# GpSimd makes a stage's first weight sums in the stage before, and junctions take their second half in another order

## The reference

```python
h = rms_norm(x, g_pre_mix) * (1 + scale1) + shift1
proj = h @ w_in                               # keys, values, queries, Fourier and conv inputs, gates
merged = sum(sigmoid(gate_b) * (branch_b @ w_br_b) for b in four branches)
x = x + gate1 * rms_norm(merged @ w_out, g_post_mix)
h = rms_norm(x, g_pre_mlp) * (1 + scale2) + shift2
x = x + gate2 * rms_norm(square(relu(h @ w1)) @ w2, g_post_mlp)
```

## Time and profile before

| what | value |
|---|---|
| median of 3 runs | 4097.98 us (4097.63 to 4100.86) |
| profiled execution | 4095.34 us, span 4093.4 us |
| TensorE busy | 3808.4 us, 93% |
| VectorE busy | 1895.3 us, 46% |
| GpSimd busy | 1026.2 us, 25% |
| ScalarE busy | 833.0 us, 20% |
| mean granted TensorE clock | 0.972 of full |

### The profile page before, as it was taken

How to read it: one execution, slowest core, us unless ns; L and a number is a source line. 1 busy time by engine, 2 the same in 40 slices (tenths; PEclk the granted TensorE clock), 3 DMA queues, 4 the chain that set the end, 5 groups by cost and what they waited for, 6 DMA issues and landing times. The chain is left out here.

```text
span 4093.4 us, 47789 instructions
## 1 busy us (share of the span) xinstructions
PE 3808.4 (93%) x18222; PEld 2592.6 (63%) x18222; DVE 1895.3 (46%) x3491; ACT 833.0 (20%) x1685; POOL 1026.2 (25%) x876
## 2 busy tenths in 40 slices
PE   6978969999989989999998999999999999979998
PEld 5866735555465557555554555555787777768887
DVE  3345332222322266787544566655225655144445
ACT  2123221111111155211213000001213511220001
POOL 1301200000014211223332223232152034434443
PEclk9988989999999999999999999999999999999999
DMA  5410179999811100122221232221110012212221
GB/s 204 178 69 16 63 289 393 395 391 395 328 36 52 47 11 8 55 91 87 88 90 41 93 116 111 103 103 52 47 63 31 10 63 75 90 62 83 83 88 57
DMA packets 72014, 476.64 MB, mean 116 GB/s; under 512 B 8240, under 2 KB 9648, under 8 KB 18288
## 3 DMA queue, kind: packets, MB, share of 16 engines
q1 hardware_dynamic: 68576, 462.86, 29.9%
q0 software_dynamic: 2640, 8.65, 0.7%
q10 hardware_dynamic: 576, 2.10, 0.1%
HBM read 469.38 MB, written 4.19 MB: 116 GB/s over the span
## 5 line engine op out<-in xcount | busy, mean ns | idle before, releaser
L921 PE MATMUL ps<-projected,weight_ring 128*128 128x384 f32 (+1 forms) x672 | 245.8, 521 | 0.0
L3410 PE MATMUL ps<-projected,weight_ring 128*128 128x384 f32 (+1 forms) x768 | 223.0, 434 | 1.2 <-DVE mlp_u L3608 0.6
L2322 DVE SCALAR_TENSOR_TENSOR sb_x_all<-ps,sb_modulation_ada,sb_x_all 128x512 f32<-128x512 f32 x144 | 106.5, 750 | 244.4 <-PE ps L2158 214.8
L921 PEld LDWEIGHTS ps<-projected,weight_ring 128*128 128x128 f32 x672 | 127.7, 190 | 106.1 <-issue 45.9
L3410 PEld LDWEIGHTS ps<-projected,weight_ring 128*128 128x128 f32 x768 | 144.8, 190 | 62.5 <-issue 3.0
L3410 PE MATMUL ps<-projected,mlp_weight_sums 128*128 128x384 f32 x512 | 176.4, 488 | 0.0
L1304 DVE TENSOR_REDUCE attention_shift<-ps 128x1 f32<-128x768 f32 (+1 forms) x160 | 130.9, 846 | 77.8 <-PE ps L1192 77.5
L1192 PE MATMUL ps<-projected 64*128 64x256 f32 (+1 forms) x576 | 136.9, 531 | 25.2 <-DVE projected L1333 15.1
L2844 DVE SCALAR_TENSOR_TENSOR projected<-projected,sb_vectors 128x497 f32<-128x497 f32 (+26 forms) x270 | 157.9, 650 | 1.6
L2704 PE MATMUL ps<-projected,gates_weight_sums 128*128 128x384 f32 (+1 forms) x512 | 151.9, 440 | 5.0 <-POOL gates_weight_sums L2984 5.0
L3410 PE MATMUL ps<-h2b,weight_ring 128*128 128x384 f32 (+1 forms) x512 | 151.0, 439 | 4.9 <-ACT h2b L834 4.9
(11 more groups left out here) (664 smaller groups left out, 7765.8 us busy)
## 6 DMA issues: line engine op xcount, KB each, us to landing
weight_ring<-w_stream SPq DMA_DIRECT2D x218, 1024.0 KB, 4.9
expert_weights<-w_moe SPq DMA_DIRECT2D x125, 1024.0 KB, 22.3
weight_ring<-w_moe SPq DMA_DIRECT2D x40, 1024.0 KB, 23.6
h2b<-w_moe SPq DMA_DIRECT2D x33, 1024.0 KB, 24.0
weight_ring<-w_stream SPq DMA_DIRECT2D x16, 512.0 KB, 3.7
weight_ring<-w_stream SPq DMA_DIRECT2D x16, 384.0 KB, 3.2
sb_x_all<-xT SPq DMA_DIRECT2D x1, 3072.0 KB, 11.9
tokens<-h_tokens ACTq DMA_DIRECT2D x4, 512.0 KB, 9.6
```

What stands on the lines that cost most here:

```text
L921: ins = nc.tensor.matmul(core.ps[:, 2 * slot + half, 0:n], w_of(k), h_of(k)[:, a:a + n], start=(first and k == 0), stop=(last and k == chu ...
L2322: v.scalar_tensor_tensor(core.x[:, k, NCTX:T], ps[:, bank, :], core.mods["ada"][:, 40 + k, 1:2], core.x[:, k, NCTX:T], ALU.mult, ALU.add). ...
L3410: ins = nc.tensor.matmul(acc, wq[:, k, :], bq[:, k, :], start=(first and k == 0), stop=(last and k == 3), skip_group_check=True)
```

## The change

GpSimd's first weight sums of `project`, `out` and `mlp` are made by the end of the stage before, in a buffer that outlives it: one unit for `project` and `out`, two for `mlp` (into chunks 9 to 14 of `pr`, for which other buffers of `out` and of the MLP's junction move). The stage that follows starts its own sums at unit 1 (at unit 2 in the MLP, without a wait for products until unit 4), and waits on counts shifted by that. `modulate_side` now stands before unit 2's sums and their weights' arrival. In every junction four adds of half 1 stand before half 0's norms instead of two; in the MLP the totals of half 1 stand before both `x_second` products, and all eight norms of half 1 before the first column sum.

```diff
@@ Junction.vector_begin
-        self.adds(dve, 1, 0, 2)
+        self.adds(dve, 1, 0, 4)
         for k in range(KD):
             self.norm(dve, 0, k)
-        self.adds(dve, 1, 2, KD)
+        self.adds(dve, 1, 4, KD)
@@ project_phase
                 jn.modulate_side(pool)
+            if ahead is not None:
+                weight_quarters(pool, ahead, stream.arrived(pool, len(units)), sums_ready, 0)
@@ gates_phase
-        sw = ph.sb("weight_sums", [P, 2, 4, 4, P])
...
                     .then_inc(m15_out, 1)
+            pool.wait_ge(products, 7 * (len(jobs) - 1))
+            weight_quarters(pool, sw[:, 0], stream.arrived(pool, 2 * len(jobs) + len(mods)), s_ready, len(jobs))
             for r in (1, 0):
@@ seven_phase
             for i in range(U):
-                w = stream.arrived(pool, i + min(burst * i, len(mods)))
-                if i >= 2:
-                    pool.wait_ge(products, 7 * (i - 1))
-                weight_quarters(pool, sw[:, i % 2], w, s_ready, i)
+                if i >= made:
+                    w = stream.arrived(pool, i + min(burst * i, len(mods)))
+                    if i >= 2:
+                        pool.wait_ge(products, 7 * (i - 1))
+                    weight_quarters(pool, sw[:, i % 2], w, s_ready, i - made)
                 pool.wait_ge(m1_out, i + 1)
...
+            for j in range(2 if ahead is not None else 0):
+                weight_quarters(pool, ahead[:, j], stream.arrived(pool, U + j), s_ready, U - made + j)
...
+            def sums(i, count):
+                if i >= made:
+                    pe.wait_ge(s_ready, 4 * (i - made) + count)
@@ mlp_phase
+        def weight_sums(i, k):
+            return (made if i < 2 else sw)[:, i % 2, k]
...
             jn.gate_gains(pool)
-            for i in range(units):
+            jn.modulate_side(pool)
+            for i in range(2, units):
                 w = stream.arrived(pool, i + min(max(i - 1, 0), len(mods)))
-                if i == 2:
-                    jn.modulate_side(pool)
-                if i >= 2:
+                if i >= 4:
                     pool.wait_ge(products, done(i - 2, 7))
...
             x_first(0, w0, lambda k: jn.normal(pe, 0, k))
+            jn.x_totals(pe, 1, 0, 1)
             x_first(1, w1)
-            jn.x_totals(pe, 1, 0, 2)
+            jn.x_totals(pe, 1, 1, KD)
             x_second(0, w0, lambda k: jn.normal(pe, 0, 4 + k))
-            jn.x_totals(pe, 1, 2, KD)
             x_second(1, w1)
...
-            for k in range(6):
+            for k in range(KD):
                 jn.norm(dve, 1, k)
             for j in range(2):
                 jn.normal(dve, j, 3)
             next(h_sums)
-            for k in range(6, KD):
-                jn.norm(dve, 1, k)
             for j in range(2):
                 jn.normal(dve, j, KD - 1)
             next(h_sums)
@@ second_block
+                prj = ExitStack()
+                sw = sb("weight_sums", [P, 2, 4, 4, P], prj)
...
-                project_phase(core, f"project_tokens{layer}", h, units, scaled=not last, join=join)
+                project_phase(core, f"project_tokens{layer}", h, units, scaled=not last, join=join,
+                              ahead=sw[:, 0])
...
+                sw = sb("gate_sums", [P, 2, 4, 4, P], mg)
...
+                made = pr[:, 9:17, :].rearrange("p c t -> p (c t)")[:, 0:32 * P].rearrange(
+                    "p (j i k m) -> p j i k m", j=2, i=4, k=4)
                 seven_phase(core, f"out{layer}", merged, span[0], n,
                             [(h[:, 2 * i, :], h[:, 2 * i + 1, :], False, 1.0) for i in range(4)],
-                            sums.rearrange("p (i k m) -> p i k m", i=3, k=4), tail=squares)
+                            sums.rearrange("p (i k m) -> p i k m", i=3, k=4), tail=squares, sw=sw, made=1, ahead=made)
```

More of the change, by code:

```diff
@@ L924, in feature_job, with project_phase @@
     return ins
-def project_phase(core, name, h, units, scaled=False, join=None):
+def project_phase(core, name, h, units, scaled=False, join=None, ahead=None):
     nc, stream = core.nc, core.stream
@@ L944, in project_phase @@
             early = sum(job[0] == "T" and job[4] < TILES // 2 for _, job in jobs)
+        sums_ready = ph.sem("weight_sums_ready") if ahead is not None else None
         owner = [0 if j < early else j % 2 for j in range(len(jobs))]
@@ L2620, in _, with gates_phase @@
                                         ALU.add).then_inc(high_out, 1)
-def gates_phase(core, name, layer, h, pr, merged, branches, span, mods=()):
+def gates_phase(core, name, layer, h, pr, merged, branches, span, sw, mods=()):
     nc, ps, stream = core.nc, core.ps, core.stream
@@ L3121, in add, with seven_phase @@
                 .then_inc(self.added, 1)
-def seven_phase(core, name, b, lo, n, units, th=None, conv=None, mods=(), burst=0, heads=None, tail=None):
+def seven_phase(core, name, b, lo, n, units, th=None, conv=None, mods=(), burst=0, heads=None, tail=None,
+                sw=None, made=0, ahead=None):
     nc, ps, stream = core.nc, core.ps, core.stream
@@ L3214, in _ @@
                     bg.turn(pe)
-                pe.wait_ge(s_ready, 4 * i + 1)
+                sums(i, 1)
                 pe.wait_ge(t_ready, 1)
@@ L3223, in _ @@
                     bg.turn(pe)
-                pe.wait_ge(s_ready, 4 * i + 3)
+                sums(i, 3)
                 pe.wait_ge(t_ready, 2)
@@ L3240, in _ @@
                 pe.wait_ge(m5_out, i + 1)
-                pe.wait_ge(s_ready, 4 * i + 4)
+                sums(i, 4)
                 product(z, s[:, 3], right(4, 1), False, True)
@@ L3326, in _, with mlp_phase @@
                     bg.add(dve)
-def mlp_phase(core, h, out, span, th, tail, hid, m1, join, mods=()):
+def mlp_phase(core, h, out, span, th, tail, hid, m1, join, made, mods=()):
     nc, ps, stream = core.nc, core.ps, core.stream
@@ L3436, in z_first @@
                     pe.wait_ge(z_out, i - 1)
-                product(banks(i)[2], sw[:, i % 2, 0], left(b, 0, lo + n), True, False)
+                product(banks(i)[2], weight_sums(i, 0), left(b, 0, lo + n), True, False)
             def y_first(i, w):
                 up, b, t, lo, ready, made = sides(i)
-                pe.wait_ge(s_ready, 4 * i + 3)
+                if i >= 2:
+                    pe.wait_ge(s_ready, 4 * i - 5)
                 pe.wait_ge(ready, made + 2)
@@ L3457, in y_second @@
                 pe.wait_ge(ready, made + 3)
-                product(banks(i)[1], sw[:, i % 2, 2], t[:, 1], False, False)
+                product(banks(i)[1], weight_sums(i, 2), t[:, 1], False, False)
             def z_second(i, w):
@@ L3462, in z_second @@
                 pe.wait_ge(m5_out, i + 1)
-                pe.wait_ge(s_ready, 4 * i + 4)
-                product(banks(i)[2], sw[:, i % 2, 3], left(b, 4, lo + n), False, True)
+                if i >= 2:
+                    pe.wait_ge(s_ready, 4 * i - 4)
+                product(banks(i)[2], weight_sums(i, 3), left(b, 4, lo + n), False, True)
             def y_third(i, w):
@@ L3926, in second_block @@
                 merged = sb("merged", [P, KD, T], mg)
+                sw = sb("gate_sums", [P, 2, 4, 4, P], mg)
                 gates_phase(core, f"gates{layer}", layer, h, pr, merged,
[L3928 removed]
+                            [(DQ, 4), (GQ, 4), (UF, 3), (UC + 3, 3)], span, sw, () if last else mod_units("mod0", 8, 24))
                 dump(f"merged{layer}", merged)
                 n = span[1] // 2
[L3931 to L3932 removed]
+                sums = pr[:, 17:23, :].rearrange("p c t -> p (c t)")[:, 0:12 * n]
+                squares = (pr[:, 4, span[0]:T], pr[:, 5:7, span[0]:T])
+                made = pr[:, 9:17, :].rearrange("p c t -> p (c t)")[:, 0:32 * P].rearrange(
+                    "p (j i k m) -> p j i k m", j=2, i=4, k=4)
                 seven_phase(core, f"out{layer}", merged, span[0], n,
                             [(h[:, 2 * i, :], h[:, 2 * i + 1, :], False, 1.0) for i in range(4)],
[L3935 removed]
+                            sums.rearrange("p (i k m) -> p i k m", i=3, k=4), tail=squares, sw=sw, made=1, ahead=made)
         cols = span[1]
```

22 lines of the change are left out of this document (11 added, 11 removed).

## The result

The changed kernel takes 4069.25 us (median of 4 runs, 4067.72 to 4071.29), the kernel before 4097.81 (4 runs, 4096.33 to 4100.86). The ratio is 0.9923, interval [0.991, 0.9935]. On the 4097.98 us that the prediction started from, that ratio is 4066.4 us (4061.1 to 4071.3 by the interval). The direction was right and most of the places too. The gain is larger than the range (4067 to 4085) allowed: by 0.6 us, which is within the noise, while the 10 us to the forecast of 4076 are not. The profiled executions are 4068.01 us (span 4066.1) against 4095.34 (4093.4): 27.3 us.

A forecast was written before the change was run, and what follows sets the result against it. TensorE, busy 93% of the span, was taken as the bound, so only its waits could be won. Terms 4.85 + 2.05 + 5.9 + 7.4 + 0.8 + 1.6 + 1.5 - 2.4 = 21.7 us gave 4076 us, range 4067 to 4085.

The forecast's parts named there:

- term of 3.25: Head of `project0`: without the wait for GpSimd's sums the third product starts 3.25 us earlier.
- 1.6 for the third product: Head of `project0`: with no idle time before it, the third product escapes the half clock, 1.6 us more gained.
- term of 2.05: Head of `out0`: the third product starts at 2133.1 instead of 2135.21, counted as 2.05 us gained.
- which stays: Head of `out0`: the second product (3.15 us) begins at the low clock, and this was taken to remain.
- 5.9 forecast: Head of `out1`: 4.6 us from waits gone plus 1.3 from the third product's clock, together 5.9 us gained.
- forecast 2.4: Tail of `out1`: GpSimd's eight sums made ahead end after the stage's old end, 2.4 us lost.
- rival on the tails: Tails of the out stages: sums at 2.77 us each and half-clock opening matmuls make the kernel slower, 4103; chance 0.03.
- 14.1: First MLP junction: norm to norm 10.8 us unheld, 14.1 with four sums each holding a VectorE operation about 0.8.
- bounds 0 to 1.2 lost: `project_tokens1`: norms start 1.2 us late, but the eighth multiply comes about when it came; taken as 0.
- No relief: Second MLP junction: GpSimd still makes eight sums at the start, only for other units, so 0 gained from them.
- I take half: First sum products of both MLPs: half the low-clock cost counted as gained, 0.8 us in the first, 1.5 in the second.
- more comes back: Rival: high clock from both MLPs' first sum product (2.3 us), adds slipping past unit 2's sums (3.3); 4071, chance 0.13.

The follow-up runs named there:

- own_sums1: The changed kernel, but `out1` makes no sums ahead and the second MLP forms those of units 0 and 1 at its start; 4067.48 us.
- hold: The changed kernel, but GpSimd forms the sums of units 2 and 3 only after the last product of units 0 and 1; 4062.51 us.
- again: A second execution of the unmodified changed kernel, for its trace; 4067.45 us.
- sums_alone: The changed kernel with the old order in all junctions, the sums still made ahead; 4080.91 us, ratio 0.9952 to the kernel before.
- order_alone: The kernel before with only the new order of the junctions, no sums made ahead; 4085.98 us, ratio 0.9963 to the kernel before.
- three_adds: `hold` with three adds of half 1 ahead of the norms instead of four, in all junctions; 4057.83 us.

## Why the prediction was off, step by step

**Heads.** `project0` became 5.0 us shorter in this pair of executions, 4.85 were forecast. But 1.7 of it is clock that before's second execution did not lose; the wait itself is worth 3.3. So the term of 3.25 is right, and that the 1.6 for the third product came too was luck. `out0`: the term of 2.05 is right where the first product is at the low clock on both sides: in `own_sums1` the third product starts at 2129.56, 8.17 us after the first, against 10.20, 2.03; what was won of it is the wait of the earlier trace rows and a little. I took the low clock there as given ("which stays"); in the changed kernel and those that share its program up to there it was there in full, in part or not at all, and `gates0` and `out0` together fell by 2.2 to 6.6 us, 4.9 in the profiled pair. That the gain came out larger than the sum is luck as far as this term goes. `out1`: 6.3 measured without the tail (358.6 to 352.3), 5.9 forecast.

**Tails.** 2.2 us in `out1` (forecast 2.4), 0 in `out0` (0). All sixteen sums took 1.26 to 1.28. The low clock behind the wait, which I had only in the rival on the tails, came in `out1`'s tail in one of the two executions (5.46 against 2.91).

**First MLP.** Forecast 8.2, measured 8.5, and two of its parts were wrong in opposite ways. The start of the norms came 6.4 us earlier (6.2). Norm to norm fell by 0.9 (1.7): I had made 14.1 out of VectorE's adds held by four sums, but with the new order these cost nothing (`hold`), and 1.7 of the 14.92 is the low clock of a first product that now waits 3.71 us. The pair of sum products gave 1.6 us, of which I had taken half.

**project_tokens1.** Forecast 0 with bounds 0 to 1.2 lost; it gained 1.2. This is a wrong sign: I saw that the eighth multiply would come when it had come, and missed that the job before it no longer halted at the seventh. Its price lay outside the bounds that I gave. That the sums cost nothing there is true only with the order; alone they cost 2.4.

**Second MLP.** Forecast 3.1, measured 5.9 (6.8 in `again`). The sum products gave 2.8 us (6.51 to 3.72), of which 1.5 was taken; norm to norm gave 1.9 (12.79 to 10.86) for 1.6; 0.5 is an early wait of unit 1 that went. "No relief" from the sums was nearly right (`sums_alone` 0.5).

**What failed, then**, is first the step "I take half", the price of the clock at the sum products, twice too small, by 2.1 us in all; `order_alone` and `sums_alone` show that the order decides it in full. The sentence on the Trainium skill (TensorE: Matmul & The Clock Gate, What's actually happening), by which activity releases the clock, pointed the right way at these products. Second, `project_tokens1`, 1.2 us, a halt that I had not seen. Third, `out0`, 2.8 us, where what I took as fixed was not. The norm to norm of the second MLP and the wait of unit 1 make 0.8. Together 6.9 of the 7.9 us by which the six stages beat the sum. The rival "more comes back" (4071) was the nearest, right in its clock part and wrong in its other: `hold`, where the adds meet no sums, shows that adds that slip past unit 2's sums would have brought nothing.

## What to carry to other kernels

Work made ahead for an engine is worth its place only if it leaves the contended stretch: in the first MLP moving eight sums out gave 7.5 us, in the second eight others moved in at once and gave 0.5, until a wait held them back (6.8, or 6.0 against the second execution). Where two engines run dense side by side, find the gap in which the helper meets nothing, and wait for that. And before costing a held operation, look whether the consumer has a gap at all: in the first junction, with the new order, TensorE had none between its first product and the last total, so neither faster adds nor earlier squares could count; with the old order it had one, and the same held adds cost 1.6 us.

## What the runs showed of the hardware

The low clock costs by where it falls: 1.7 us for a product of eight matmuls of 384 columns in the junctions (4.51 against 2.82), 2.6 at the head of `out0` (5.46). Its fall is not told by the wait just ahead: 2.71 us came before either level in the same code, though all twenty sum-product pairs that came after 1.5 to 1.6 us were high and all six after 3.2 to 3.8 us low. Behind waits of 3.02 to 3.04 us the twelve opening matmuls of the second MLP took 2.91 us four times, 4.37 and 4.53 once each, and 5.46 once. Over the whole span the mean granted clock was 0.972 in the two traces of before, 0.975 in the two of after, 0.977 in `hold` and `three_adds`.

A VectorE operation with both inputs in SBUF that runs beside a GpSimd sum of two SBUF inputs takes about 1 us more: 1.48 against 0.42 (L876, 256 columns, after and `hold`), 1.62 against 0.55 (384, `sums_alone`). The sum itself goes from 1.26 to 1.44 and to 1.58. Beside L3301, with one input in PSUM, both keep their 0.42 and 1.26.
